# Two unrolled layers, w_ada tiles on four column groups, and the next modulation read inside the feed-forwards

## What is computed

```python
def layer_forward(x, c, ...):
    sh1, sc1, g1, sh2, sc2, g2, sh3, sc3, g3 = ada_modulation(c, w_ada, b_ada)
    h = modulate(rms_norm(x, norm_ffn1), sh1, sc1)
    x = x + 0.5 * g1 * swiglu(h, w_ffn1_in, w_ffn1_out)
    h = modulate(rms_norm(x, norm_mix), sh2, sc2)
    u = h @ w_in                     # four mixers: SSD, RG-LRU, HGRN2, MLA
    ...
    x = x + g2 * (y @ w_out)
    h = modulate(rms_norm(x, norm_ffn2), sh3, sc3)
    x = x + 0.5 * g3 * swiglu(h, w_ffn2_in, w_ffn2_out)
```

## Time and profile before

| | |
|---|---|
| time, median of 3 runs | 2104.76 us (2100.86 to 2105.81) |
| span of the profiled execution | 2103.4 us |
| busy: PE, PEld, DVE, ACT, POOL | 1930.5, 1602.5, 978.3, 581.7, 187.6 us |
| read from memory | 264.68 MB, 128 GB/s over the span |
| records of the w_ada matmuls (L698) | 1152, 244.3 us busy |

### The profile page before, as it was taken

One profiled execution on the slowest core, in us unless ns is written; L12 is line 12 of the kernel. 1 busy time (PEld: TensorE's weight loads), 2 busy tenths in 40 slices (PEclk: granted clock), 3 DMA queues, 4 the chain that ended last, 5 costly groups with the idle time before them and its releaser, 6 DMA issues. The chain is left out here.

```text
span 2103.4 us, 28262 instructions
## 1 busy us (share of the span) xinstructions
PE 1930.5 (92%) x11420; PEld 1602.5 (76%) x11420; DVE 978.3 (47%) x1749; ACT 581.7 (28%) x768; POOL 187.6 (9%) x337
## 2 busy tenths in 40 slices
PE   6999998998869998999979999989987689989998
PEld 3599997776636557999946999967766365679998
DVE  0534442576575435444205444336756664244442
ACT  1333331042312213333113333211422122133331
POOL 0000003500223000000000000043003120000000
PEclk9999999998667998999989999999986689989999
DMA  7935445421011452445296544463201116424442
GB/s 248 300 121 161 150 146 152 132 94 43 16 34 48 157 187 85 152 137 162 71 284 222 160 160 139 137 174 113 92 23 25 34 47 200 160 93 136 153 159 68
DMA packets 260360, 272.15 MB, mean 129 GB/s; under 512 B 10892, under 2 KB 255090, under 8 KB 260216
## 3 DMA queue, kind: packets, MB, share of 16 engines
q1 hardware_dynamic: 246432, 250.42, 37.3%
q0 software_dynamic: 12032, 19.63, 3.7%
q10 hardware_dynamic: 1752, 0.18, 0.1%
HBM read 264.68 MB, written 5.50 MB: 128 GB/s over the span
## 5 line engine op out<-in xcount | busy, mean ns | idle before, releaser
L744 PE MATMUL bank<-hT_r,ring_r 128*128 128x320 f32 x1408 | 439.1, 312 | 0.0
L744 PEld LDWEIGHTS bank<-hT_r,ring_r 128*128 128x128 f32 x1408 | 268.6, 191 | 0.0
L698 PE MATMUL bank<-ring,csT 128*32 128x256 f32 x1152 | 244.3, 387 | 21.7 <-DMA ring<-in_w_ada_dram 21.7
L698 PEld LDWEIGHTS bank<-ring,csT 128*32 128x32 f32 x1152 | 120.2, 112 | 141.3 <-DMA ring<-in_w_ada_dram 22.6
L817 PE MATMUL bank<-hT,ring 128*128 128x320 f32 x736 | 211.7, 448 | 9.8 <-DVE hT L1465 9.8
L744 PE MATMUL bank<-big_r,ring_r 128*128 128x320 f32 x704 | 217.7, 309 | 0.0
L1452 DVE TENSOR_TENSOR ring_r<-ring,lat_pages_r 128x2048 fp32r<-128x2048 f32 (+1 forms) x64 | 142.3, 2225 | 135.6 <-ACT lat_pages_r L1212 135.5
L817 PEld LDWEIGHTS bank<-hT,ring 128*128 128x128 f32 x736 | 144.1, 198 | 70.8 <-issue 16.4
L743 PE MATMUL bank<-gates_r,lat_pages_r 128*128 128x320 f32 x640 | 197.3, 308 | 0.0
L742 PE MATMUL bank<-hT_r,lat_pages_r 128*128 128x320 f32 x640 | 196.9, 308 | 0.0
L1212 ACT ACTIVATE lat_pages_r<-ring 128x2048 fp32r<-128x2048 f32 (+1 forms) x64 | 119.1, 1861 | 120.0 <-PE bank L744 59.4
(11 more groups left out here) (496 smaller groups left out, 3242.9 us busy)
## 6 DMA issues: line engine op xcount, KB each, us to landing
ring<-in_w_ffn_in_dram SPq DMA_DIRECT2D x88, 1024.0 KB, 5.8
ring<-in_w_ada_dram SPq DMA_DIRECT2D x72, 1024.0 KB, 5.5
ring<-in_w_ffn_out_dram SPq DMA_DIRECT2D x32, 1024.0 KB, 5.2
ring<-in_w_in_dram SPq DMA_DIRECT2D x20, 1024.0 KB, 5.5
ring<-in_w_ffn_out_dram SPq DMA_DIRECT2D x16, 768.0 KB, 4.4
lat_pages<-in_cache_mla_latent_dram POOLq DMA_DIRECT2D x128, 64.0 KB, 2.1
ring<-in_w_out_dram SPq DMA_DIRECT2D x8, 1024.0 KB, 5.0
ring<-in_w_in_dram SPq DMA_DIRECT2D x2, 1040.0 KB, 5.7
```

The source lines that it names most:

```text
L698: ins = mm(bank[banks[a // ADA_ROWS]][row:row + 32, at:at + 256], csT[:, k * NQ:k * NQ + 32], w[:, k], start=k == 0, stop=k == KD - 1)
L744: return mm(out, w_l, x_h, start=False, stop=stop)
```

## The change

The loop is unrolled into one block. Semaphores are no longer cleared; each wait adds the counts of the layers before. A tile of `w_ada` is now two of the eight row chunks by all 1024 columns of a group: still 1 MB, in runs of 4 KB where they were 1 KB. Its eight matmuls go to four strips in turn, `csT` being loaded into another 32-column group of PE each time. Only groups 0 and 1 of the first layer stand ahead of its feed-forward. Its groups 2 to 4 (12 tiles) are placed in the input half of its first feed-forward, and groups 0 to 4 of the second layer (20 tiles) in that of the first layer's second feed-forward: one `w_ada` tile behind each feed-forward tile i from 2 on in the ring, and its matmuls behind step j = i. Groups 5 to 8 stay where they were. The parameters of the second layer are loaded by POOL, and its constants, first norm sum and first three tiles are prepared in that feed-forward too.

```diff
-            for a in range(ADA_A):
-                ada(a)
...
+        def ada_in_ffn(l, w):
+            if w == 0:
+                return [(0, g, q) for g in (2, 3, 4) for q in range(KA)] if l == 0 else []
+            return [(l + 1, g, q) for g in range(5) for q in range(KA)] if l + 1 < depth else []
+        def ada_after(l, w):
+            steps = list(range(2, KF))
+            return dict(zip(steps, ada_in_ffn(l, w)))
...
+            def ffn(l, w, win, wout):
+                after = ada_after(l, w)
+                for i in range(FT):
...
+                    if i in after:
+                        ada(*after[i])
+            for g in range(2):
+                for q in range(KA):
+                    ada(0, g, q)
+            for l in range(depth):
+                ffn(l, 0, "w_ffn1_in", "w_ffn1_out")
...
+                for n, (src, chunks, width) in enumerate(tl):
+                    if n >= RING:
+                        sp.wait_ge(*FREE[n - RING])
+                    sp.dma_start(slot(n, chunks, width), src).then_inc(slot_loaded[n % RING], 16)
...
+                        for k in range(2 * q, 2 * q + 2):
+                            for r in range(4):
+                                ins = mm(bank[ADA_BANK[pair]][32 * r:32 * r + 32, c0:c0 + 256], csT[:, k * NQ:k * NQ + 32],
+                                         w[:, k - 2 * q, 256 * r:256 * r + 256], start=k == 0, stop=k == KD - 1)
...
                                 ins.then_inc(gu_done, 1)
+                                if j in ada_tiles:
+                                    ada(*ada_tiles[j])
```

More of the change, by code:

```diff
@@ L351, in trunk @@
[L351 to L364, removed]
@@ L481, in slot @@
+        tl = tiles()
         def slot(n, chunks, width):
@@ L508, in _ @@
+                pool.dma_start(pages[0:1, :], A["page_table"].rearrange("(o a) b -> o (a b)", o=1)).then_inc(table_loaded, 16)
+                pool.wait_ge(table_loaded, 16)
                 pool.wait_ge(lru_zeroed, 1)
[L510 to L529, removed]
-                                               rows_in[i][0:L, (4 * g + k) * P:(4 * g + k + 1) * P],
-                                               c("ident", L)[:, 0:L])
-                        ins.then_inc(turned, 1)
-                        n += 1
@@ new lines, in _, with here, high @@
+                for i, (t0, L) in enumerate(TC):
+                    for g in range(2):
+                        for k in range(4):
+                            ins = pe.transpose(bank[2 * i + g][0:L, k * P:(k + 1) * P], xT[:, 4 * g + k, t0:t0 + L], c("ident"))
+                        ins.then_inc(y_turned, 1)
+            @block.scalar
+            def _(ac):
+                o = Order(ac, act_step)
+                f = nc.scalar.activation
+                def here(s, n):
+                    return in_layer(l, s, n)
+                ac.wait_ge(c_loaded, 32)
+                o.go(f(hT[0:NQ, 4:8, 0:256], hT[0:NQ, 0:4, 0:256], ACT.Silu), c_ready)
+                load_params(ac, 0)
+                for l in range(depth):
+                    def high(l_, w, i):
+                        n = T_FFN[l_, w, i]
+                        if i >= HI:
+                            ac.wait_ge(*FREE[T_FFN[l_, w, i - HI]])
+                        elif w:
+                            ac.wait_ge(*FREE[T_FFN[l_, 0, FT - HI + i]])
+                        elif l_:
+                            ac.wait_ge(*FREE[T_FFN[l_ - 1, 1, FT - HI + i]])
@@ new lines, in ffn, with square_after, ada_copy @@
+                            if nl < depth:
+                                square_after(w, 2 * mp)
+                                square_after(w, 2 * mp + 1)
+                    def square_after(w, k):
+                        ac.wait_ge(*here(fo_used, w * KD + k + 1))
+                        o.go(f(sqx[:, k], xT[:, k], ACT.Square), squared)
+                    def ada_copy(l_, pair, rows):
+                        n = 256 * len(ADA_PAIRS[pair])
+                        ac.wait_ge(*in_layer(l_, ada_used, KA * (ADA_PAIRS[pair][-1] + 1)))
+                        if pair in (1, 2):
+                            ac.wait_ge(*in_layer(l_, ada_turned, pair))
+                        o.go(f(rows[:, 0:n], bank[ADA_BANK[pair]][:, 0:n], ACT.Copy), ada_copied)
@@ new lines, in exponents @@
+                    def exponents(l_):
+                        ac.wait_ge(*in_layer(l_, ssd_act_in, 1))
+                        o.go(f(aneg, alog, ACT.Exp))
+                        o.go(f(e0, e0, ACT.Exp))
+                        o.go(f(e1, e1, ACT.Exp))
+                        o.go(f(sp[1][:, 12:14], sp[1][:, 12:14], ACT.Exp, scale=-1.0), ssd_act)
+                    if l == 0:
+                        ac.wait_ge(x_taken, 6)
+                        for k in range(KD):
+                            o.go(f(sqx[:, k], xT[:, k], ACT.Square), squared)
+                        norm_root(0)
+                        exponents(0)
+                        ada_copy(0, 0, ada_rows_a)
+                        high(0, 0, 0)
+                        high(0, 0, 1)
+                        modulate(0)
+                        high(0, 0, 2)
+                        high(0, 0, 3)
+                    else:
+                        norm_root(0)
+                        modulate(0)
+                        high(l, 0, 3)
```

1115 lines of the change are left out of this document (578 added, 537 removed).

## The result

The changed kernel takes 2190.99 us (median of 4 runs, 2184.94 to 2197.06), against 2103.91 us for the kernel before in the runs beside it: a ratio of 1.0419, 95% interval 1.0396 to 1.0442. It is 4% slower; 2187 was forecast. Its profiled execution took 2184.94 us, with a span of 2183.3.

The account below looks back on a forecast made before the run. PE, busy 92% of the span, was taken as the bound. Costs of 260.9 us less savings of 178.9 made 82.0 slower; 2103.4 + 82.0 + 1.4 = 2186.8, said as 2187, range 2145 to 2235.

Parts of the forecast that it names:

- The refill: Layer 0 feed-forwards: PE waits (holds) for tiles issued only at a pair's end, 13.1 us each typically, 203.1 together.
- The clock: After each of 16 waits for late feed-forward tiles, PE restarts at half speed, losing 2.3 us: 36.8 together.
- The price of a w_ada tile: On PE, four strips at once make a tile 0.9 us, before 3.64; 16 tiles outside the waits cost 14.4.
- The first head: Start to first silu: fewer tiles loaded, then serial preparation; first silu at 76.6 against 109.24, saving 32.6 us.
- The second head: Last residual of layer 0 to first silu of layer 1: everything prepared, passage 20.3 us, saving 78.3.
- The mixers: First w_ada tile of the mixers to w_out: cheaper tiles save 33 us a layer, bounds 20 and 41.6; both layers 66.
- the walk through the ring: Mixers: following PE's order through tile loads put w_out at 733 instead of 766.46, 33 us saved of at most 41.6.
- the moved work: Layer 0 feed-forward: norm sums 3.4 us and some 28 small transposes 3.2 added to PE, 6.6 together.
- The sum: Whole kernel: costs of 260.9 us less savings of 178.9, net 82.0 us slower.
- The holds don't happen: Rival for layer 0 feed-forwards: the late tiles arrive in time, kernel faster at 1961 us; chance 0.07.
- Four strips gain nothing: Rival on PE: 16 tiles cost 2.7 us more each, the mixers save nothing, time 2296 us; chance 0.07.
- the clock stays low: Rival for layer 0 feed-forwards: PE keeps half clock through each pair, losing 14 us, not 2.3; 2374 us; chance 0.04.

Follow-up runs that it names:

- The run one step earlier: The thin spread with its w_ada tile behind even steps 2 to 20 instead of odd ones, in ring and on PE: 2274.7 us, ratio 1.0823.
- the thin spread: Changed kernel with one w_ada tile a pair behind odd steps, each layer's groups 2 to 4 in its own first feed-forward: 1973.6 us, ratio 0.9391.

## Why the prediction was right, step by step

**The refill.** Right in place, number and size. Idle time in the 16 holds adds up to 186.8 us, and a tile of 1.07 ahead of each makes it 203.9; the forecast was 203.1. The run one step earlier and the two with loads or matmuls left out show that the loads' place in the ring makes them. The Trainium skill (DMA: Bandwidth & Descriptors, "Anatomy of one DMA") gave an estimate of 11.6 for a hold; 12.9 was measured, and the landings of the earlier trace rows were the better source.

**The clock.** Right. After the 16 holds PE works for 72.3 us at half clock, which loses 36.2; the forecast was 36.8, or 2.3 a hold. The range of a single hold is wide, 1.4 to 2.8, and the two cases of the earlier trace rows, 1.9 and 4.0, don't say why 2.3 should be the mean: that the estimate between them came out so well is in part luck.

**The price of a w_ada tile.** 1.07 alone and 3.66 for four in a row; 0.9 forecast. In the first feed-forward its 12 tiles take 12.85 us. The Trainium skill (TensorEngine Tiling (Array Packing), "Key Properties") says that tiles of the array work independently and that a change of mode drains the engine. The trace agrees with the first. For the second, a lone tile is only 1.07 - 0.92 = 0.15 dearer than one in a row, and the pair of 15.28 us in the thin spread is 1.20 longer than before, so at most 1.20 - 0.92 = 0.28 can be a drain; the 0.56 that the prediction weighed isn't there in that size.

**The first head**, 39.9 and not 32.6. Three steps were put too long: the norm sums ran at full clock (4.57 and not 9.1), DVE took the parameters while PE still waited to transpose the modulation, so it had 15.0 us to do behind that and not 18.7, and the first silu came 10.3 after the first matmul and not 11.4. These make 9.3. The transposes, with their wait for ACT, took 4.4 and not 2 (and the forecast's own terms up to there add up to 46.0, not 46.5). Part of the 39.9 is this one execution: in the profiles of the seven versions with the same head the first silu stands at 69.4 to 74.4, a gain of 35 to 40. PE:

```profile
35.11 4.57 PE L728 MATMUL bank<-sq,cst 128*128 128x320 f32 x16
...
59.09 0.61 PE L746 MATMUL bank<-hT_r,lat_pages_r 128*128 128x320 f32 x1 [15.01 <-DVE gates_r L1552]
```

**The second head**, 78.6 against 78.3, by taking the passage from a place where the kernel already had everything prepared.

**The mixers**, 31.6 against 33, but by other steps. The window over the 16 tiles alone (first) has 18.27 us and not 14.4; the others are the stretch from the first `w_ada` tile to `w_out`, before and after, with all engines (columns as in rows 2):

```profile
690.00:800.00 110.00, 18.27 (x256) 8.17 (x256) 0.89 0.50 162
```

```profile
675.46:766.46 91.00, 88.26 (x458) 51.23 (x458) 38.19 (x57) 17.58 (x29) 0.00 (x0) 0.97 0.54 174
```

```profile
729.84:789.22 59.38, 52.11 (x459) 33.35 (x458) 38.99 (x63) 17.15 (x29) 18.88 (x38) 0.92 0.63 223
```

So PE does 55.98 - 18.27 = 37.7 less there. What was given back is 4.6 us of new idle time (59.38 - 52.11 = 7.3 us idle against 2.7) and 1.5 of a lower clock (0.92 against 0.97) and rounding; the walk through the ring had 8.6 for loads alone. Leaving those loads out gave 1.6. The sum was right because two errors met: that is luck.

**What was left out.** The stretch from `w_out` on is 4.4 longer. Its four tiles and then the feed-forward's land later than before, ACT waits in `high`, and the square that PE needs for the norm sum stands behind it. With the late loads left out this wait is gone (the ACT row of that experiment). ACT and PE, after:

```profile
804.43 1.91 ACT L1249 ACTIVATE conv_r<-ring 128x2048 fp32r<-128x2048 f32 x1 [4.87 <-DMA ring<-in_w_ffn_in_dram]
```

```profile
803.29 4.47 PE L1206 MATMUL bank<-hT,ring 128*128 128x320 f32 x16
810.09 0.81 PE L728 MATMUL bank<-sq,cst 128*128 128x320 f32 x2 [2.33 <-ACT sq L1254]
810.73 6.16 PE L1206 MATMUL bank<-hT,ring 128*128 128x320 f32 x16
...
817.27 0.97 PE L1206 MATMUL bank<-hT,ring 128*128 128x320 f32 x3
```

The same place before:

```profile
780.46 4.47 PE L1190 MATMUL bank<-hT,ring 128*128 128x320 f32 x16
...
785.31 4.47 PE L1190 MATMUL bank<-hT,ring 128*128 128x320 f32 x16
```

The groups of 16 came every 4.85 us. Now one comes after 7.44, by the wait, and the next after 6.54, at a lower clock: 2.6 + 1.7 = 4.3 of the 4.4. No step of the prediction had asked what stands behind ACT's `high` at this place. In the second feed-forward the gaps (117.8, less 1.2 idle before), the tiles (21.4) and the clock (23.6) make 161.7 of the 167.7, so the moved work is 6.0 us, close to the 6.6 that were put for it.

**The sum.** Holds, clock and tiles, the terms that decide, were right one by one. The total is nearer than all its parts: 7.3 us too little for the first head stand against 4.4 left out behind `w_out` and the small misses of the rest.

**The rivals.** *The holds don't happen* was given 1961; where they were removed, the times are 1973.6 and 1971.2, of which 32 tiles at 1.07 instead of 0.9 explain 5. *Four strips gain nothing* and *the clock stays low* fell: a tile took 1.07 us, and the clock was at half for 2.9 to 5.7 us after a hold.

## What to carry to other kernels

When a load is put into a ring that is already tuned, write down for each tile which slot it needs and when that slot comes free: with slots freed in pairs, the tile that stands one ring length ahead decides whether the load is issued a pair early or only when it is needed, and the mean use of memory tells nothing of it. Here, with five slots, one extra tile a pair behind both members made no hold, and the rest was spread over more feed-forwards. A cheaper matmul and a better place are worth little one by one and a lot together: placement without packing was 0.4% slower than before, packing with the wrong place 4.2% or 8.2% slower, both in the right place 6% faster.

## What the runs showed of the hardware

Four strips of 32 columns multiply at the same time at full rate: 16 records of 128x32 by 256 columns take 1.07 us, 64 take 3.66, where one strip took 3.64 and 11.50. It makes no difference whether neighbouring matmuls go to different strips or two by two to the same one (1.07 and 1.09 us): work for one strip does not hold up the matmuls of another behind it in the order. After gaps of 10 and of 12 us alike the granted clock was at half, for 3.4 to 5.6 us of solid matmuls after the one and 2.9 to 5.7 after the other, and then full again: the price, 2.1 and 2.3 us on average, hardly depended on the gap, though single gaps cost from 1.4 to 2.8.
